# Second stack's attention: the pooled products ahead of the turning in each step, and the halves of ScalarE's chunk splits in other steps

## The reference

```python
def second_block(x, positions, g_pre_mix, w_in, w_pool, pool_scale, w_out, g_post_mix,
...
        a_out = pool_mixer(u_pool, w_pool[l], pool_scale[l])
        b_out = dsa_attention(q, k, v, iq, ik, iw, topk)
        mix = jnp.concatenate([a_out, b_out], axis=-1) @ w_out[l]
...
def dsa_attention(q, k, v, iq, ik, iw, topk):
...
        s = jnp.einsum('bqhd,bqkhd->bqhk', qb.astype(jnp.float32), kg.astype(jnp.float32)) * (HEAD_DIM ** -0.5)
        s = jnp.where(valid[:, :, None, :], s, -jnp.inf)
        p = jax.nn.softmax(s, axis=-1)
        o = jnp.einsum('bqhk,bqkhd->bqhd', p, vg.astype(jnp.float32))
```

## Time and profile before

| | us |
|---|---|
| median of 3 runs | 2460.05 (2459.33 to 2461.67) |
| profiled execution, its own time | 2455.17 |
| its span, first to last instruction | 2453.4 |
| TensorE busy | 2394.1 (98% of the span) |
| the loop in the first layer, S(2) to the first product behind it | 57.05 (1396.12 to 1453.17) |
| the loop in the second layer, the same | 59.07 (1992.21 to 2051.28) |

### The profile page before, as it was taken

How to read it: one execution, slowest core, us unless ns; L and a number is a source line. 1 busy time by engine, 2 the same in 40 slices (tenths; PEclk the granted TensorE clock), 3 DMA queues, 4 the chain that set the end, 5 groups by cost and what they waited for, 6 DMA issues and landing times.

```text
span 2453.4 us, 28925 instructions
## 1 busy us (share of the span) xinstructions
PE 2394.1 (98%) x11498; PEld 1937.7 (79%) x11498; DVE 1362.2 (56%) x1976; ACT 895.8 (37%) x1299; POOL 349.9 (14%) x270
## 2 busy tenths in 40 slices
PE   8999999999999999999999999999999999999997
PEld 6877888888887788888876878888886877888886
DVE  7775433445777543344578876344357975633433
ACT  4555332234355533223432354223243244321331
POOL 2002000001200200000246521000012832000002
PEclk9999999999999999999999999999999999999998
DMA  4311222222231222222221221222221211222221
GB/s 158 107 57 69 98 91 103 91 98 86 102 109 56 74 102 87 103 94 89 91 91 69 69 84 59 103 93 95 102 104 57 87 52 70 81 91 103 91 97 51
DMA packets 33181, 215.56 MB, mean 88 GB/s; under 512 B 4145, under 2 KB 4401, under 8 KB 8113
## 3 DMA queue, kind: packets, MB, share of 16 engines
q1 hardware_dynamic: 33072, 214.08, 24.4%
HBM read 211.97 MB, written 2.10 MB: 87 GB/s over the span
## 4 chain that ended last, share of the span: by engine, by line
PE 89%; DVE 7%; ACT 2%; issue 1%; POOL 1%; DMA 0%; SPq 0%; POOLq 0%; DVEq 0%; ACTq 0%
PE ps L426 81%; DVE wl L366 1%; PE ps L2225 1%; PE ps L2178 1%; DVE gl L648 1%; PE ps L2249 1%; PE ps L2239 1%; PE ps L1389 1%; PE ps L606 1%; PE ps L1413 1%; PE ps L309 1%; PE ps L1376 1%; ACT wh L360 0%; PE ps L2228 0%; DVE x L1340 0%
## 5 line engine op out<-in xcount | busy, mean ns | idle before, releaser
L426 PE MATMUL ps<-gh,wh 128*128 128x512 f32 x1488 | 589.4, 396 | 13.6 <-DVE gl L648 11.0
L426 PE MATMUL ps<-gh,wl 128*128 128x512 f32 x1488 | 581.0, 390 | 0.0
L426 PE MATMUL ps<-gl,wh 128*128 128x512 f32 x1488 | 580.9, 390 | 0.0
L426 PE MATMUL ps<-hh,wh 128*128 128x512 f32 x1456 | 575.1, 395 | 3.0 <-ACT arena L964 1.1
L360 ACT ACTIVATE wh<-wr 128x2048 fp32r<-128x2048 f32 x184 | 351.1, 1909 | 594.9 <-PE ps L426 594.5
L426 PE MATMUL ps<-hh,wl 128*128 128x512 f32 x1456 | 567.3, 390 | 0.0
L426 PE MATMUL ps<-hl,wh 128*128 128x512 f32 x1456 | 567.0, 389 | 0.0
L366 DVE TENSOR_TENSOR wl<-wr,wh 128x2048 fp32r<-128x2048 f32 x168 | 387.1, 2304 | 277.8 <-ACT wh L360 275.5
L426 PEld LDWEIGHTS ps<-gh,wh 128*128 128x128 f32 x1488 | 279.3, 188 | 82.1 <-DVE gl L648 13.5
L426 PEld LDWEIGHTS ps<-hh,wh 128*128 128x128 f32 x1456 | 272.9, 187 | 68.3 <-issue 8.0
L426 PEld LDWEIGHTS ps<-gh,wl 128*128 128x128 f32 x1488 | 279.5, 188 | 59.7
(11 more groups left out here) (264 smaller groups left out, 2445.8 us busy)
## 6 DMA issues: line engine op xcount, KB each, us to landing
wr<-in_weights SPq DMA_DIRECT2D x195, 1024.0 KB, 4.8
out_yt<-x SPq DMA_DIRECT2D x8, 256.0 KB, 2.0
x<-in_xt SPq DMA_DIRECT2D x3, 512.0 KB, 7.9
wr<-in_weights SPq DMA_DIRECT2D x2, 512.0 KB, 5.8
arena<-in_gates SPq DMA_DIRECT2D x2, 512.0 KB, 7.7
arena<-in_embed SPq DMA_DIRECT2D x2, 512.0 KB, 5.3
par<-in_params_b SPq DMA_DIRECT2D x2, 274.0 KB, 2.7
x<-in_xt SPq DMA_DIRECT2D x2, 256.0 KB, 4.1
```

The costliest lines, as they stand in the source:

```text
L426: done = pe.matmul(out, stationary, moving, start=(first and n == 0), stop=(last and n == 2), skip_group_check=True)
```

## The change

In TensorE's program the pooled part of a step moves ahead of the step's `turn`. In ScalarE's program the halves of the split of `B_POOL + 1` move from steps 1 and 2 to steps 0 and 3, and those of `B_ATT` from steps 9 and 10 to 11 and 12. Nothing is added or left out.

```diff
@@ ScalarE, the loop over s
             untangle(s)
-            for c, steps in ((B_POOL + 1, (1, 2)), (B_ATT, (STEPS // 2 + 1, STEPS // 2 + 2))):
+            for c, steps in ((B_POOL + 1, (0, 3)), (B_ATT, (STEPS // 2 + 3, STEPS // 2 + 4))):
                 if s in steps:
                     split_high_part(act, mem, sem, c, steps.index(s))
@@ TensorE, the loop over s
             if s + 2 < STEPS:
                 scores(s + 2)
-            turn(s)
             if s in POOLED_STEPS:
                 pooled_part(4 + POOLED_STEPS.index(s))
+            turn(s)
             if s:
                 weigh(s - 1)
```

## The result

The change makes the kernel **slower by 7.8 us**: 2467.48 us (median of 6 runs, 2465.30 to 2469.26) against 2459.69 us of the kernel before beside it (median of 6, 2456.95 to 2461.67). The ratio is 1.0031, with a 95% interval of 1.0021 to 1.0042. The forecast was 2464.0 (4.0 us slower) in a range of 2457.0 to 2467.0; it gave 0.30 to a slower kernel and 0.59 to a change too small to tell.

A forecast was written before the change was run, and what follows sets the result against it. TensorE, busy 98% of the span, was taken as the bound, so only shortening its waits pays. Step 0 +0.2, heads -0.3 and tails +4.1 summed to +4.0 us: 2464.0, range 2457.0 to 2467.0.

The forecast's parts named there:

- Step 5, part 8: Loop head: the pooled part waits 2.05 us for GpSimd's low split, slow clock costs 1.45, S(8) comes at +10.8.
- Rival 1: Clock holds through step 5, so 1.45 us come back in each layer: +1.1, 2461.1 us; chance 0.17.
- T(4) and T(12): Turnings of steps 4 and 12 start without waiting for VectorE's scaling; T(4)'s 2.18 us wait goes.
- 0.1 in step 0: P(4), right behind S(2), waits for `keep_pooled(1)`: 0.1 us in each layer.
- Two terms put at nothing: Parts 10 and 14 wait zero, at most 0.6 us each; P followed by T costs what T followed by P does.
- T(14)'s place: Loop tail: step 14's turning starts 31.05 us behind S(8) in the first layer, 30.7 in the second.
- the second rival: VectorE is not held in step 14; T(14) waits 1.4 and 2.1 us, no clock falls: -1.8, 2458.3 us; chance 0.13.
- T(14) waits 3.5 us: Second layer's step 14: wait for the scaling held under GpSimd's pieces, 1.4 us from order alone; first layer 3.8.
- I take 1.0 of the 0 to 1.45: Slow clock behind T(14)'s wait, to the loop's end, put at 1.0 us in each layer.
- tails: S(8) to the loop's end: 36.0 us in the first layer (+3.2), 35.7 in the second (+0.9).
- heads: S(6) to S(8): 10.8 us against 10.98 and 10.93, -0.3 us over both layers.
- the fourth rival: Everything costs its upper bound: full clock fall after step 14, part 14 waits 0.6: +6 to +7, 2466.5 us; chance 0.20.

The follow-up runs named there:

- `pair_high` first: The change, with `pair_high` ahead of the exponents in ScalarE's steps 5, 9 and 13; 2466.31 us, ratio 1.0022 to the kernel before.
- the order alone: The kernel before with TensorE's new order only, ScalarE's splits staying in steps 1, 2, 9, 10; 2454.83 us, ratio 0.9981.
- splits alone: The kernel before with only ScalarE's splits moved as in the change, TensorE's order as before; 2458.34 us, ratio 0.9986.
- the kernel with products ahead in 3 and 11: The kernel before, with splits in steps 0, 1, 8, 9 and pooled products ahead of the turning in steps 3 and 11 alone; 2448.85 us, ratio 0.9950.
- the kernel with all products ahead: The change's TensorE order, pooled products ahead in all twelve steps, with ScalarE's splits in steps 0, 1, 8, 9; 2458.50 us, ratio 0.9991.

## Why the prediction was wrong, point by point

- **Step 5, part 8: right.** Predicted wait 2.05, measured 2.05 in both layers, clock down behind it. S(8) came at 11.04 and 11.06 instead of 10.8. Of the missing 0.25 the clock is 0.15: it costs 1.6 (11.03 against 9.44 with the same wait), where 1.45 was taken. Rival 1 did not happen in this kernel, but one layer of the run with `pair_high` first shows that it could have. One reading beside it was off: before, the low part was ready 5.7 us ahead of part 8 (2008.06 against 2013.78), not 4; no sum used it.
- **T(4) and T(12): right.** Their waits went. The 0.1 in step 0 was right as well.
- **Two terms put at nothing: right.** Parts 10 and 14 do not wait after (with the order alone part 14 does, 0.98 and 0.32), and P ahead of T adds nothing where no engine is late: S(8) to S(12) is 13.67 with `pair_high` first, for 13.62.
- **T(14)'s place: right within 0.5.** It came 31.53 and 30.85 behind S(8), for 31.05 and 30.7. The chain of held operations was as described, in the second layer by L1989 and L1990 alone: L1978 slipped by in 0.17, as the second rival has it, but both scalings were held all the same. In the first layer L2015 (1.10 for the 1.76 counted), L1978 (0.78) and L1989 (1.25) were held, and L1990 ran free right behind GpSimd's last piece.
- **"T(14) waits 3.5 us": right as a sum, wrong in its parts.** The wait is split over W(12) (1.38) and T(14) (2.83, 2.17), which make 4.21 and 3.55. That the sum came out near is due to VectorE, whose end sets T(14)'s start either way; the prediction let W(12) go by unnoticed: it counted `pair_low` into VectorE's chain and forgot that W waits for it too. The same wait stands in small ahead of W(8) (0.44), and makes S(8) to S(12) 13.97 and 13.95 where 13.62 was counted. Most of the 0.5 by which the first layer's T(14) is late is this.
- **The failed step: "I take 1.0 of the 0 to 1.45" for the clock behind T(14).** It cost 2.2 and 2.8 us, beyond the top of the range given; the error of 1.2 and 1.8 is 3.0 of the 4.4 us that the sum of +4.0 lacks against the loops' +8.4. The mechanism (a clock that falls behind this wait) was right, its price was not. The upper end 1.45 came from one place, T(4), where the slow stretch ended within step 5. Behind the second layer's T(14) the rows above have the clock at 0.50 and 0.51 from 2058.0 to 2064.5. It need not have two waits ahead of it for that: behind the single waits of 2.75 (splits alone) and 3.51 and 3.07 (`pair_high` first) T(14) to the end took 6.84, 6.72 and 6.73, and 5.55 behind the single 2.08. So the clock's price behind such a wait lay between 1.5 and 2.8 us in the tails. Why it differs between waits of about the same length (2.8 behind the 2.17, 1.5 behind the 2.08, 1.6 or nothing behind the 2.05 of the heads) is open. With an upper end of 3.0 (all of it slow: 6.98 against 4.02) and nothing else changed, the fourth rival would have been +9.
- **The sum.** Heads +0.2 for -0.3, tails +5.06 and +2.95 for +3.2 and +0.9, step 0 +0.2 for +0.2: +8.4 for +4.0. The measured median difference is 7.8.
- **Sign and chances.** The slow clock costs 8.2 us of the loops after (2.2 + 2.8 behind T(14), 1.6 twice in the heads) and cost about 4.4 before (1.45 in each head, and 34.88 - 31.26 - 2.18 = 1.44 in the second tail, by the working of the prediction). So of the 8.4 about 3.9 are clock and 4.5 waits. The gain on T(4) and T(12) is real and is eaten by waits elsewhere, as the forecast had it; the range was too narrow because one number for the clock was carried over from one kind of place to another.

The Trainium skill ("SBUF — State Buffer", section "Who interferes with whom") has VectorE's `tensor_scalar` in a 2-port mode and GpSimd exclude each other, and `tensor_reduce` stay free. The rows above agree: L1976 took 0.41 with GpSimd beside it, and L1989 and L1990 took 1.21 to 1.35 under GpSimd's pieces and 0.35 without.

## What to carry to other kernels

An edit that covers a wait moves the lateness on; follow the producer that is late (here GpSimd's four pieces and the VectorE operations that they hold) until it meets slack, and price every wait on the way, with all the semaphores of each waiting instruction. Test the halves of a double change apart: here each was a gain and the two together a loss. One figure for the clock behind a wait of TensorE was too little here: the waits of 2.05 to 3.51 us cost nothing to 2.8 us, so take the whole range that the traces show. Move covering work only to the consumer that is late (steps 3, 4, 11, 12 here): moved everywhere, it made the consumers late that were not.

## What was not expected of the hardware

- The clock after a wait of 2.05 fell in one layer and held in the other of the same execution, with the same work ahead (0.65 and 1.00 in the stretches behind it). Behind 2.52 it held as well (T(10) of the kernel with products ahead in 3 and 11, whose stretch 1390 to 1470 has 1.00), while behind 2.62 at the same T(10) of the kernel with all products ahead it fell to 0.50.
- With nine products of no use in the pause ahead of T(14), where TensorE otherwise stood still for 2.2 to 2.8 us, the clock is 1.00 behind it, and the loops are 5.1 us shorter (3.4 us by the medians).
- An operation of VectorE on two elements a row (L1978) took up to 1.26 us under GpSimd's pieces, for 0.17 otherwise, as long as one on 256.
